# Constants in two transfers, the first projection chunk loaded and split ahead of the last modulation chunks, and a router and a final norm that work tile by tile

## The reference

```
for l in 0, 1:
    m = silu(c) @ w_mod[l] + b_mod[l]              # six rows of 1024: shift, scale, gate, twice; latent and context
    h = rmsnorm(x, g_norm1[l]) * (1 + m[1]) + m[0]
    p = h @ w_in[l]                                # split into memory, attention and convolution columns
    x = x + m[2] * (mixers(p) @ w_out[l])
    h = rmsnorm(x, g_norm2[l]) * (1 + m[4]) + m[3]
    x = x + m[5] * (dense_swiglu(h) if l == 0 else moe_swiglu(h))
out = rmsnorm(x, g_final)                          # latent tokens alone

moe_swiglu: logits = h @ w_r + b_r (1024 x 8); softmax; the top 2 of 8 experts; weighted sum of their SwiGLUs
```

## Time and profile before

| what | value |
|---|---|
| median of 3 runs | 1561.84 us (1553.97 to 1564.56) |
| the profiled execution | 1566.26 us |
| its span, first to last instruction | 1564.5 us |
| PE busy | 1418.2 us, 91% of the span |
| DVE, ACT, POOL busy | 61%, 40%, 22% |
| share of the chain that ended last | PE 67%, DVE 9%, POOL 8%, ACT 7%, DMA 3% |
| mean granted TensorE clock | 0.958 of full speed |

### The profile page before, as it was taken

The page is one execution under the profiler, slowest core; times in us unless marked ns, Lnnn a source line. Parts: engine busy times, 40 slices in busy tenths (PEclk is TensorE's granted clock), DMA queues, the critical chain, the costliest instruction groups (busy, mean ns, idle before and its releaser), DMA issues.

```text
span 1564.5 us, 20098 instructions
## 1 busy us (share of the span) xinstructions
PE 1418.2 (91%) x7474; PEld 1127.8 (72%) x7474; DVE 958.6 (61%) x1376; ACT 633.3 (40%) x1020; POOL 348.9 (22%) x272
## 2 busy tenths in 40 slices
PE   5699999898979999999997999685999999999996
PEld 2587778555438888888885989375788888878884
DVE  2843545555654444435347765744878988887985
ACT  2324323356121110001004534433767676676773
POOL 0219999910010000000001699700000000000000
PEclk9899889799989999999998999797999999999999
DMA  8244333585112322322231322006879779777940
GB/s 359 106 188 154 117 135 109 187 294 193 54 54 81 108 87 101 108 74 101 101 114 53 109 85 89 18 0 282 340 295 370 276 289 361 284 285 315 340 183 27
DMA packets 30303, 267.03 MB, mean 171 GB/s; under 512 B 3360, under 2 KB 3360, under 8 KB 4256
## 3 DMA queue, kind: packets, MB, share of 16 engines
q1 hardware_dynamic: 30240, 266.15, 44.9%
HBM read 265.09 MB, written 1.05 MB: 170 GB/s over the span
## 4 chain that ended last, share of the span: by engine, by line
PE 67%; DVE 9%; POOL 8%; ACT 7%; issue 5%; DMA 3%; ACTq 0%; DVEq 0%; SPq 0%
PE ps L480 31%; PE ps L864 13%; PE ps L884 6%; POOL sb_arena L1900 5%; PE ps L750 4%; POOL sb_arena L1903 3%; PE ps L493 3%; DMA sb_arena<-in 2%; PE ps L834 2%; PE ps L510 1%; DVE sb_rows_n L1595 1%; PE ps L843 1%; DMA sb_arena<-mod 1%; PE ps L628 1%; PE ps L662 1%
## 5 line engine op out<-in xcount | busy, mean ns | idle before, releaser
L480 PE MATMUL ps<-sb_h_hi,sb_w_hi 128*128 128x512 f32 (+1 forms) x640 | 244.9, 383 | 10.0 <-DVE sb_h_lo L1376 9.8
L480 PE MATMUL ps<-sb_h_lo,sb_w_hi 128*128 128x512 f32 (+1 forms) x640 | 242.3, 379 | 0.0
L480 PE MATMUL ps<-sb_h_hi,sb_w_lo 128*128 128x512 f32 (+1 forms) x640 | 242.2, 378 | 0.0
L1900 POOL TENSOR_SCALAR sb_arena<-sb_arena,sb_small 128x512 f32<-128x512 f32 (+1 forms) x120 | 186.2, 1551 | 11.8
L480 PEld LDWEIGHTS ps<-sb_h_hi,sb_w_hi 128*128 128x128 f32 x640 | 122.9, 192 | 34.7 <-DVE sb_h_lo L1376 10.6
L864 PE MATMUL ps<-sb_egu_lo,sb_h_lo 128*128 128x512 f32 (+1 forms) x384 | 142.8, 372 | 0.0
L480 PEld LDWEIGHTS ps<-sb_h_hi,sb_w_lo 128*128 128x128 f32 x640 | 122.6, 192 | 22.3
L480 PEld LDWEIGHTS ps<-sb_h_lo,sb_w_hi 128*128 128x128 f32 x640 | 123.0, 192 | 21.6
L1903 POOL TENSOR_TENSOR sb_arena<-sb_arena 128x512 f32<-128x512 f32 (+1 forms) x120 | 134.7, 1123 | 10.0
L1746 DVE TENSOR_TENSOR sb_egu_lo<-sb_arena,sb_con_r 128x1024 fp32r<-128x1024 f32 x98 | 115.3, 1218 | 31.1 <-ACT sb_con_r L1213 31.0
L1375 DVE CAST sb_w_hi<-sb_arena 128x2048 fp32r<-128x2048 f32 (+1 forms) x40 | 49.0, 1225 | 136.0 <-PE ps L480 126.8
(11 more groups left out here) (308 smaller groups left out, 2957.4 us busy)
## 6 DMA issues: line engine op xcount, KB each, us to landing
sb_arena<-experts SPq DMA_DIRECT2D x90, 1536.0 KB, 8.5
sb_arena<-mod SPq DMA_DIRECT2D x48, 1024.0 KB, 5.0
sb_arena<-in SPq DMA_DIRECT2D x24, 1024.0 KB, 4.8
sb_arena<-gate SPq DMA_DIRECT2D x11, 1024.0 KB, 4.8
sb_arena<-up SPq DMA_DIRECT2D x11, 1024.0 KB, 4.8
sb_arena<-out SPq DMA_DIRECT2D x8, 1024.0 KB, 4.8
sb_arena<-down SPq DMA_DIRECT2D x8, 1024.0 KB, 4.8
sb_arena<-down SPq DMA_DIRECT2D x4, 768.0 KB, 4.2
```

What stands on the lines that cost most here:

```text
L480: ins = pe.matmul(o, left[a], right[b], start=(k == first and n == 0), stop=(k == final and n == len(PRODUCTS) - 1))
L1900: g.tensor_scalar(p, u, w[:, j:j + 1], None, ALU.mult)\
```

## The change

The fields of `con` get a new order: `eps`, `one`, `fold`, `ones` first, so that every later field lies four columns further on. The first 132 columns are loaded where all of `con` was; the other 2696 follow the last of the first eight modulation chunks under a semaphore of their own (`tables_loaded`). Chunk "mk" moves to place 6 of the ring's list, ahead of modulation chunks 6 and 7, and the gate weights go just before it. ACT makes the leading bits of the gate weights and of "mk" between modulation rows 5 and 6, DVE only the remainders. The squares of `X` follow the second modulation row instead of the fourth. The rounding of `pick` and the masks moves on DVE from the first microseconds to the start of layer 0's `gate_rows`. The router takes each tile of `h` as it comes, into two banks. In the final norm ACT squares each quarter and also multiplies it with the gain, PE sums the quarters as they come, DVE multiplies with the reciprocal quarter by quarter, and each quarter has its own transfer.

```diff
-NORM_AFTER = 4
+NORM_AFTER = 2
+LEAD_FIRST = 6
...
-CONST, NCONST = fields([("ident", P), ("ones", P), ("mask_f", P), ("mask_b", P), ("cos", SEQ), ("sin", SEQ),
-                        ("reset", T), ("pick", NH * 2 * P), ("before", P), ("slots", P), ("order", NE), ("eps", 1), ("one", 1), ("fold", 2)])
+CONST, NCONST = fields([("eps", 1), ("one", 1), ("fold", 2), ("ones", P), ("ident", P), ("mask_f", P), ("mask_b", P), ("cos", SEQ), ("sin", SEQ),
+                        ("reset", T), ("pick", NH * 2 * P), ("before", P), ("slots", P), ("order", NE)])
+NCONST_FIRST = CONST["ident"][0]
...
         chunks = [("mod", 0, i) for i in range(FIRST_MOD)]
+        chunks.insert(LEAD_FIRST, ("in", 0, IN_ORDER[0]))
         for l in range(DEPTH):
             for n in IN_ORDER:
-                chunks.append(("in", l, n))
+                if (l, n) != (0, IN_ORDER[0]):
+                    chunks.append(("in", l, n))
...
                 if n == 1:
-                    sp.dma_start(con[:, :], A["con"]).then_inc(sem_con, 16)
+                    sp.dma_start(con[:, 0:NCONST_FIRST], A["con"][:, 0:NCONST_FIRST]).then_inc(sem_con, 16)
                     sp.dma_start(X[:, :, :], A["x"].rearrange("p (k t) -> p k t", k=KD)).then_inc(sem_x, 16)
-                if (n == RING) if l == 0 else (kind == "in" and i == IN_ORDER[0]):
+                if n == FIRST_MOD + 1:
+                    sp.dma_start(con[:, NCONST_FIRST:], A["con"][:, NCONST_FIRST:]).then_inc(sem_tables, 16)
+                if kind == "in" and i == IN_ORDER[0]:
...
-            sp.wait_ge(*dve_done.at("final"))
-            sp.dma_start(A["out_0"].rearrange("p (k t) -> p k t", k=KD), h2).then_inc(sem_out, 16)
-            sp.wait_ge(sem_out, 16)
+            for q in range(4):
+                sp.wait_ge(*dve_done.at(("final", q)))
+                sp.dma_start(A["out_0"].rearrange("p (k t) -> p k t", k=KD)[:, 2 * q:2 * q + 2], h2[:, 2 * q:2 * q + 2, :])\
+                  .then_inc(sem_out, 16)
+            sp.wait_ge(sem_out, 64)
...
-                pe.wait_ge(*act_done.at(("h", 1, 1, KD - 1)))
-                o = open_bank("logits")
+                o = [open_bank(("logits", b)) for b in range(2)]
                 w = par("w_router").rearrange("p (k e) -> p k e", k=KD)
-                for b in range(2):
-                    for k in range(KD):
-                        ins = pe.matmul(o[:, b * NE:(b + 1) * NE], h2[:, k, b * P:(b + 1) * P], w[:, k, :],
+                for k in range(KD):
+                    pe.wait_ge(*act_done.at(("h", 1, 1, k)))
+                    for b in range(2):
+                        ins = pe.matmul(o[b][:, 0:NE], h2[:, k, b * P:(b + 1) * P], w[:, k, :],
                                         start=(k == 0), stop=(k == KD - 1))
...
             for i in range(FIRST_MOD):
+                if i == LEAD_FIRST:
+                    act.wait_ge(sem_gw[0], 16)
+                    f(wg_hi[:, :, :], w_gates, ACT.Copy).then_inc(*act_done.tick("lead_gates"))
+                    lead(("in", 0, IN_ORDER[0]))
                 modulation_rows(0, i)
...
-            act.wait_ge(*dve_done.at("x_final"))
-            f(experts[:, 0, 0:KD * SEQ].rearrange("p (k t) -> p k t", k=KD), X[:, :, CTX:T], ACT.Square)\
-                .then_inc(*act_done.tick("final_sq"))
+            for q in range(4):
+                act.wait_ge(*dve_done.at(("x_final", q)))
+                f(x_squared[:, 2 * q:2 * q + 2, :], X[:, 2 * q:2 * q + 2, CTX:T], ACT.Square).then_inc(*act_done.tick(("final_sq", q)))
+                for k in (2 * q, 2 * q + 1):
+                    ins = f(x_gained[:, k, :], X[:, k, CTX:T], ACT.Copy, scale=par("g_final")[:, k:k + 1])
+                ins.then_inc(*act_done.tick(("final_gain", q)))
             f(spare, eps, ACT.Sqrt)
...
             def gate_rows(l):
 
                 R = GATE_ROWS
+                if l == 0:
+                    dve.wait_ge(sem_tables, 16)
+                    for name in ("pick", "mask_f", "mask_b"):
+                        v.tensor_copy(rounded(name), field(con, CONST, name))
...
-            for k in range(KD):
-                ins = v.scalar_tensor_tensor(h2[:, k, :], X[:, k, CTX:T], par("g_final")[:, k:k + 1], rstd[:, 0:SEQ],
-                                             ALU.mult, ALU.mult)
-            ins.then_inc(*dve_done.tick("final"))
+            for q in range(4):
+                dve.wait_ge(*act_done.at(("final_gain", q)))
+                pair = slice(2 * q, 2 * q + 2)
+                v.tensor_tensor(h2[:, pair, :], x_gained[:, pair, :], rstd[:, 0:SEQ].unsqueeze(1).to_broadcast([P, 2, SEQ]),
+                                ALU.mult).then_inc(*dve_done.tick(("final", q)))
```

44 lines of the change are left out of this document (28 added, 16 removed).

## The result

| | before | after |
|---|---|---|
| median of 10 runs each | 1562.15 us (1553.97 to 1566.64) | 1550.53 us (1545.18 to 1563.72) |
| ratio of after to before | | 0.993, 95% interval 0.9904 to 0.9956 |
| profiled execution | 1566.26 us | 1547.92 us |
| its span | 1564.5 us | 1546.1 us |
| mean granted TensorE clock | 0.958 | 0.961 |

The medians give 11.6 us, or 0.7%, which is within 1% and not the "faster by over 1%" that had 0.6. The time lies inside the range. The two profiled executions differ by 18.4 us, almost exactly the forecast 18.5. The rest of this document is about these two numbers.

What follows compares the result with a forecast made beforehand. PE is busy 91% of the time, so the change targets its waits in front, router and tail: 11.2 + 3.6 + 3.7 = 18.5 us off 1561.84 gives 1543.3 us, range 1534 to 1553.

Steps and rivals of the forecast that it cites:

- faster by over 1%: Whole kernel: the outcome class that the forecast alone, 15.6 us or more gained, would give; chance 0.6.
- Constants, 3.3 us: Front: 1348 KB fewer constants loaded early at 420 GB/s bring everything behind 3.3 us earlier.
- Norm earlier: Front: squares behind row 1 start PE's norm matmuls at 23.6 instead of 32.4, the reciprocal at 28.1 instead of 36.9.
- The split as the bound of the front: Front: DVE's remainders end at 39.7, behind the load and PE floor of modulation bias at 39, and set the start.
- the front is late on PE: Front rival: slow clock through the chunks or ACT's copies cut its gain to 8 or 9 us, total 1547; chance 0.2.
- Front, 11.2 us: Everything up to S: first product at 42.6 instead of 53.85, gain 11.2 us, lower end 8, upper 14.
- S: End of the front: the start of PE's first product (L480 matmul), 53.85 us before, forecast 42.6.
- Covers in layer 0: Layer 0: moved constant casts (1.0 us) and later "cg" load cost nothing, with 2.1 and 2.5 us left.
- the rival of the ring's order: Layer 0 projection: "cg" comes later than S + 26.9 and stalls PE, total 1546 or 1548; chance 0.1.
- Router, 3.6 us: Router: PE starts after the first `h` tile, 0.5 us in, and ends 3.6 us earlier; bounds 2.5 and 4.
- Tail, 3.7 us: Final norm and output: root 1.4 us earlier, products and last transfer 2.3 more, together 3.7; from 2.3 to 4.7.
- Slower by the constants' new order: Expert loop rival: moved `glead` slows PE's operand reads; gain gone from 21% slower, 1569 us at 50%; chance 0.03.

Runs made afterwards that it cites:

- kernels step by step: Kernel before plus constants in two transfers; then also norm behind chunk 2; then also new chunk order, DVE making both split halves: 1576.74, 1572.73, 1557.93 us.
- the kernel with the front alone: Kernel before with all hunks up to `gate_rows` (constants, earlier norm, chunk order, ACT's leading copies), router and tail unchanged: 1557.26 us, ratio 0.9939.
- the one with the router and tail alone: Kernel before with only the per-tile router and the final norm and output in quarters: 1556.05 us, ratio 0.9949.
- the second set: Changed kernel rerun unedited beside the kernel before: 1549.37 us against 1564.36, ratio 0.9915.
- the last kernel: Kernel before, without the change, plus first attention unit's maxima moved earlier and nine unread products ahead of layer 1's modulation chunk 1: 1553.01 us, ratio 0.9926.

## Why the prediction was right, and where it was not

- **Constants, 3.3 us.** Right: chunk 0 to chunk 1 went from 10.8 to 7.6, 3.2 us. The other 1.0 of the 4.2 between the two profiles is the first load's own start.
- **Norm earlier.** Right in kind and size. Sums at 17.9 (forecast 18.9), PE's norm products at 22.6 (23.6), the reciprocal at 27.15 (28.1), all by that 1 us early.
- **The split as the bound of the front.** This step failed. I had the floor of DMA and PE at "modulation bias at 39" and DVE's end at 39.7, and took DVE. DVE ended at 38.4, on the forecast once the earlier first load is taken off, and the bias started at 40.76, behind PE. Two terms of the other arm were mis-sized: chunk 7 landed 30.2 us behind chunk 0 instead of 28.6, and PE, which I had at its fast clock through chunk 7, had fallen to the slow one while it waited for the loads, so product and turns took 3.7 us and not 2.1. This is the rival "the front is late on PE", in part: it needed slow chunks throughout, and only the last was (in three of the five profiles the last two).
- **Front, 11.2 us.** Measured 9.2 from chunk 0 in the profiles and 8.3 to 10.3 over all profiles with this front. Within the bounds of 8 and 14. Of the forecast's 11.2, 8.8 were the earlier reciprocal (constants and norm) and 2.6 the splits, 5.8 us on DVE instead of 8.4. The first measured 9.0 in the kernels step by step (46.05 to 37.06). The second came on DVE, 5.6 us instead of 8.4, but hardly at S: with the new chunk order S moved from 37.06 to between 35.78 and 37.75. So the term that failed is the splits' 2.6.
- **Covers in layer 0.** Right: "cg" split at S + 27.3 (forecast 26.9), scan at S + 32.5 (32.2), PE without a gap; the rival of the ring's order is out, and the casts of the constants (0.96 us) cost nothing.
- **Router, 3.6 us.** Right: 3.64 from norm to gather. PE started 0.75 us into the `h` tiles instead of 0.5, and took 6.8 us for its records instead of 7.0. Nothing is taken back by loads: from gather to the first expert product it takes 9.05 us, 9.12 before. The loop's 1.4 us are not the router's either: the kernel with the front alone has the same loop (460.3 us against 459.0), and the one with the router and tail alone has the old one (459.2).
- **Tail, 3.7 us.** Right: 3.77. The root starts 3.9 us after the last add (forecast 4.1); DVE's products take 2.50 (2.5), the last 256 KB 2.7 us (2.5). The table load stood open as forecast, with no gap on either side of it: squares and gains end at 1536.67, the load starts at 1536.69, the next instruction at 1537.98. The drain of some 1380 ns that the Trainium skill (ScalarE: Activation LUTs, "What ACT_TABLE_LOAD costs") adds does not show in these rows, and by it the tail would have gained 2.3.
- **Slower by the constants' new order.** In its size out, 392 ns against 389 and nowhere near 21%. But the sign that I had named, a longer trip of the expert loop, is there: 1.4 us over the loop in every profile with the new constants, and 1.7 us more in the final sum where the tail is the old one. The sum had nothing for it. (The rival's 1569 us at 50% slower was also added up wrongly: half of 89 us on top of 1543.3 is 1588.)
- **The sum.** 16.6 us by the edits' own milestones against 18.5. The profiles' 18.4 owes 3.2 us to luck (first load 1.03, the convolution stretch 2.06, and the small rest), and the loop took 1.4 back, so that the profiled time came out at 1547.92 against a forecast of 1547.8 by errors that cancel. With the loop the edits gave 15.2 us. The medians gave 11.6 and, in the second set, 15.0. I took the profile's gain as "the same" for the median. That step is unsafe in this kernel: in all eleven profiles without an edit at the start of attention there is a stretch at half clock, and the code around it takes 241.4 to 255.4 us. By the clocks of the runs, the median of ten still depends on how many caught the long one.

What stays open is why the stretch is short in one run and long in the next with the same instructions. That it did not start without PE's waits is shown; what ends it is not. Open too is why the loop runs 1.4 us longer with the new constants.

## What to carry to other kernels

When an edit shortens one arm of a join, work out the other arm with the same care, with the clock that PE will have after its new waits; here the two arms lay 0.7 us apart in the forecast and the wrong one was taken. Measure steps from an event inside the program, not from its start. And when identical code takes 242 us in one profile and 255 in another, look at the granted clock by windows first: waits of 2 and 3 us at the start of a stage cost 9 to 12 us with what followed, as much as the front's whole reordering gave, and one moved reduction removed most of it. Last, compare stages far from the edit over several profiles: one pair showed the loop 1.4 us longer and could have been scatter, fourteen profiles tell that it is the change.

## What the runs showed of the hardware

- A wait of PE of 2 to 3 us at the start of attention was followed by some 25 to 60 us at 0.50 of the full clock in ten profiles of eleven (in one by 9 us, with a second stretch behind), although PE was 100% busy in most windows of it; without the waits the same work ran at 1.00 (280 to 370 us in the last kernel). A wait of 3.10 us ahead of the final sum was followed by 0.50 in four profiles and by 1.00 in three.
- Chunk 0 to S repeats within 0.03 us in four profiles of kernels with the old front, while the new front varies by 2 us (35.78 to 37.75 in five); there S follows the product of the chunk loaded last by 6.63 us in all five.
- The products on `x_r` in the expert loop took 389 ns in the median with the old constants and 393 with the new, and the loop 458.9 to 459.2 us against 460.2 to 460.6.
- A 1 MB load that was issued 1.5 us behind another took 7.0 to 7.8 us with 1348 KB issued 0.4 us behind it (five profiles), and 6.9 and 7.1 us with 1 MB issued 1.5 us behind it (two).
